# Four plain pairs instead of five in the first feed-forward block of a two-layer decoder trunk

## The reference, cut to what matters

```
def rms_norm(x, gain):
    y = xf * lax.rsqrt(jnp.mean(xf * xf, axis=-1, keepdims=True) + RMS_EPS)
    return (y * gain)
def swiglu(x, w_gate, w_up, w_down):
    return (jax.nn.silu(x @ w_gate) * (x @ w_up)) @ w_down
x = x + FFN_RESIDUAL * swiglu(rms_norm(x, g[0]), ffn_w_gate[layer, 0], ffn_w_up[layer, 0], ffn_w_down[layer, 0])
```

## Time and profile before

| | |
|---|---|
| median of 3 runs | 1962.5 us (1962.04 to 1962.67) |
| the profiled execution | 1962.62 us, span 1960.9 us |
| TensorE busy | 1949.4 us, 99% of the span |
| VectorE busy | 1396.1 us, 71% |
| ScalarE busy | 852.6 us, 43% |
| GpSimd busy | 525.8 us, 27% |
| the chain that ended last | TensorE 93%, VectorE 3% |

### The profile page before, as it was taken

The page is one execution under the profiler, slowest core; times in us unless marked ns, Lnnn a source line. Parts: engine busy times, 40 slices in busy tenths (PEclk is TensorE's granted clock), DMA queues, the critical chain, the costliest instruction groups (busy, mean ns, idle before and its releaser), DMA issues.

```text
span 1960.9 us, 28973 instructions
## 1 busy us (share of the span) xinstructions
PE 1949.4 (99%) x11722; PEld 1707.9 (87%) x11722; DVE 1396.1 (71%) x1881; ACT 852.6 (43%) x1231; POOL 525.8 (27%) x394
## 2 busy tenths in 40 slices
PE   9999999999999999999999999999999999999999
PEld 7999998877789999988999998877777888999997
DVE  8877776554578777768877786773458567877873
ACT  6443333535564333445433344442546345333431
POOL 1322222152222222223322322200015413322221
PEclk9999999999999999999999999999999999999999
DMA  6566663351336666534666653222200235666653
GB/s 214 151 167 167 173 170 98 119 172 54 101 117 168 168 174 166 161 119 134 178 172 171 177 158 113 97 91 91 76 1 1 86 108 162 175 179 165 179 143 106
DMA packets 110229, 265.92 MB, mean 136 GB/s; under 512 B 10129, under 2 KB 18577, under 8 KB 110097
## 3 DMA queue, kind: packets, MB, share of 16 engines
q1 hardware_dynamic: 90096, 225.72, 34.9%
q0 software_dynamic: 19856, 38.28, 12.4%
q10 hardware_dynamic: 144, 0.09, 0.0%
HBM read 259.32 MB, written 4.72 MB: 135 GB/s over the span
## 4 chain that ended last, share of the span: by engine, by line
PE 93%; DVE 3%; ACT 1%; issue 1%; DMA 1%; POOL 0%; SPq 0%; DVEq 0%
PE BANKS L657 12%; PE BANKS L659 12%; PE BANKS L658 12%; PE BANKS L579 10%; PE BANKS L581 10%; PE BANKS L580 10%; PE BANKS L710 6%; PE BANKS L711 6%; PE BANKS L712 6%; PE BANKS L1023 2%; PE BANKS L851 1%; PE BANKS L853 1%; PE BANKS L852 1%; PE BANKS L1000 1%; PE BANKS L814 1%
## 5 line engine op out<-in xcount | busy, mean ns | idle before, releaser
L579 PE MATMUL BANKS<-XH,HI 128*128 128x512 f32 x624 | 245.9, 394 | 3.9 <-DVE LO L1652 1.9
L657 PE MATMUL BANKS<-BF,ASH 128*128 128x256 f32 x876 | 248.0, 283 | 0.0
L658 PE MATMUL BANKS<-BFL,ASH 128*128 128x256 f32 x876 | 247.9, 283 | 0.0
L659 PE MATMUL BANKS<-BF,ASL 128*128 128x256 f32 x876 | 247.9, 283 | 0.0
L1652 DVE TENSOR_TENSOR LO<-RING,HI 128x1024 fp32r<-128x1024 f32 (+2 forms) x204 | 215.0, 1054 | 42.1 <-ACT HI L1159 40.7
L580 PE MATMUL BANKS<-XL,HI 128*128 128x512 f32 x624 | 243.2, 390 | 0.0
L581 PE MATMUL BANKS<-XH,LO 128*128 128x512 f32 x624 | 243.1, 390 | 0.0
L1172 ACT ACTIVATE TMP<-TMP 128x512 f32<-128x512 f32 x88 | 55.7, 633 | 411.8 <-DVE TMP L1681 411.8
L2251 POOL TENSOR_TENSOR TMP<-TMP,RSTD 128x512 f32<-128x512 f32 x88 | 131.4, 1493 | 365.3 <-ACT TMP L1172 365.3
L2243 POOL DMA_DIRECT2D ASR<-gu_dram x73 | 88.1, 1219 | 398.4 <-DMA ASR<-gu_dram 391.9
L710 PE MATMUL BANKS<-HH,DHI 128*128 128x512 f32 x496 | 194.0, 391 | 0.1
(11 more groups left out here) (249 smaller groups left out, 4866.4 us busy)
## 6 DMA issues: line engine op xcount, KB each, us to landing
RING<-gu_dram SPq DMA_DIRECT2D x174, 512.0 KB, 3.6
ASR<-gu_dram SPq DMA_DIRECT2D x146, 256.0 KB, 2.9
ASR<-gu_dram POOLq DMA_DIRECT2D x73, 512.0 KB, 6.8
DRAW<-down_dram SPq DMA_DIRECT2D x48, 512.0 KB, 3.7
RING<-oin_dram SPq DMA_DIRECT2D x32, 512.0 KB, 3.5
RING<-down_dram SPq DMA_DIRECT2D x32, 384.0 KB, 3.2
RING<-ein_dram SPq DMA_DIRECT2D x16, 512.0 KB, 3.5
RING<-oout_dram SPq DMA_DIRECT2D x16, 512.0 KB, 3.5
```

The source lines that it names most:

```text
L579: pe.matmul(PS[bank][:], HI[j][:, c], hi(k), start=(n == 0), stop=False)
L657: pe.matmul(out, w_hi[:, c], x_hi(k), start=(k == 0), stop=False)
L658: pe.matmul(out, w_hi[:, c], x_lo(k), start=False, stop=False)
L659: last = pe.matmul(out, w_lo[:, c], x_hi(k), start=False, stop=(k == 3))
```

## The change

`PLAIN[0]` goes from 5 to 4: pair 4 becomes a block pair, the forms, the weight sums and the first early part are wanted one pair sooner, and the early parts follow pairs 4 to 19 in place of 5 to 20. The written lists of ScalarE and VectorE for f == 0 lose one plain pair and are put into another order, near that of block 1. The lists of SyncE, GpSimd and TensorE follow from `PLAIN`.

```diff
-PLAIN = (5, 4, 3, 3)
+PLAIN = (4, 4, 3, 3)
@@ ScalarE, f == 0
                     form_split(f, 1)
                     h_high(0)
+                    split(7, whole)
                     silu(1, 1.0)
-                    split(7, whole)
                     form_inputs(f, 3)
                     form_split(f, 2)
+                    sums_split(first, 0)
+                    form_split(f, 3)
                     h_high(1)
-                    split(8, whole)
+                    split(2 * first, whole)
                     silu(2, 1.0)
-                    form_split(f, 3)
                     h_high(2)
-                    split(9, whole)
-                    sums_split(first, 0)
-                    silu(3, 1.0)
-                    split(2 * first, whole)
-                    h_high(3)
@@ VectorE, f == 0
                     split(6, whole)
-                    up(0)
                     form(f, 2)
                     form_split(f, 1)
+                    up(0)
+                    split(7, whole)
                     gate(1)
-                    split(7, whole)
-                    up(1)
                     form(f, 3)
                     form_split(f, 2)
-                    gate(2)
-                    split(8, whole)
                     form_split(f, 3)
-                    up(2)
-                    gate(3)
-                    split(9, whole)
+                    up(1)
                     sums_second(first)
                     sums_third(first)
-                    up(3)
+                    gate(2)
+                    up(2)
```

## The result

The changed kernel takes **1968.13 us** (median of 8 runs, 1967.25 to 1968.63), the kernel before beside it on the same chip 1962.62 us (median of 8 runs, 1962.04 to 1963.28). The ratio is 1.0027, 95% interval 1.0018 to 1.0036: slower by 5.5 us. The forecast was 1967.7. The profiled execution took 1968.36 us, its span is 1966.5 us; those of before took 1962.62 and 1960.9.

What follows compares the result with a forecast made beforehand. TensorE, busy in 99% of the span, was taken as the bound. The terms -0.8 + 3.75 + 0.25 + 0.85 + 1.1 = +5.15 us, on a median of 1962.5, gave 1967.7 us, range 1964.5 to 1970.3.

Steps and rivals of the forecast that it cites:

- The trade, -0.8: TensorE, pair 4 of block 0: 84 block-pair matmuls (10.07 us) replace 48 plain ones (10.88), worth -0.8 us.
- Unit 7, +3.75: Block 0: TensorE waits for VectorE's up(1) until 49.65 instead of 46.00, +3.65, plus 0.1 for a slower first matmul.
- the effect at 1.2: VectorE and GpSimd lock: taking them as independent would get form(2) below 1.2 us earlier, the first stall 1.2 smaller.
- Block start +0.25: Block 0's first block pair: TensorE waits for the up tile's split, until 55.35, +0.25 us with the slower first matmul.
- second product +0.85: Block 0's first block pair: second product waits for the first sums' split, ending at 57.65, +0.85 us.
- last product +1.1: Block 0's first block pair: last product starts at 66.05, set by gate(3) and a 7.41 us chain, +1.1 us.
- The clock as a rival, 1970.1: Clock falls to 1.2 GHz in the stall, unit 7's matmuls cost 2.4 us more: 1970.1 us; chance 0.12.
- the prediction's own last line: Wrong if unit 7 starts within 1 us of 46.0, the clock leaves full level, or loss lies behind 75 us.
- Block 1's price: Rival: block 0 only pays waits like block 1's at unit 7 and last product, 2.2 in all: 1963.9 us; chance 0.15.
- no stall: Rival: VectorE is never held up, up(1) ends at 44.4, only the trade is left: 1961.7 us; chance 0.07.
- The backlog: Rival: VectorE, some 4 us behind, makes the next block pair wait too, up to 1 us: 1968.7; chance 0.08.
- No further waits: TensorE, behind the first block pair's last product: no further waits up to 350 us; block 0 ends about 5 us later.

Runs made afterwards that it cites:

- experiment 4: The changed kernel with 14 matmuls, whose output nobody reads, put into TensorE's stall ahead of block 0's unit 7: 1968.01 us, ratio 1.0028.
- experiment 2: The kernel before with four plain pairs in block 0, its lists in their old order without pair 4's entries: 1969.62 us, ratio 1.0033.
- experiment 1: The changed kernel with VectorE's up(1) moved directly behind gate(1), ahead of form(3) and two form splits: 1969.37 us, ratio 1.0037.
- experiment 6: The changed kernel with block 0's ScalarE and VectorE lists reordered and mid sums ahead of the early split in all blocks: 1963.92 us, ratio 1.0005.
- experiment 7: As experiment 6, but mid sums ahead of the early split in blocks 0 and 1 only: 1962.62 us, ratio 0.9998.
- experiment 3: The kernel before (five plain pairs) with only VectorE's up(1) moved back, behind form(3) and form_split(2): 1964.42 us, ratio 1.0007.
- experiment 9: The kernel before with mid sums first in blocks 0 and 1, and block 1's unit 7 split ahead of h_high(1) and up(1): 1960.15 us, ratio 0.9983.
- experiment 5: The changed kernel with VectorE's mid sums ahead of the early weights' split in every block's first block pair: 1967.66 us, ratio 1.0024.

## Why the prediction was right

Term by term, by the prediction's own steps:

- **The trade, -0.8.** Not to be seen alone, but block 0's sum closes with it: -0.8, + 3.62 and the slower first matmul (0.1) for unit 7, + 1.61 for the low clock, + 0.56 for the last product (65.98 against 56.78 + 6 x 1.44 = 65.42) gives 5.09, as measured.
- **Unit 7, +3.75.** Right, step for step: `up(0)` was put at 38.75 and came at 38.68, `gate(1)` 42.5 and 42.41, `up(1)` 48.9 and 48.79, unit 7 49.65 and 49.62. It took the turns of VectorE and GpSimd to get there: the form's first row at 35.01 lasts 1.0 longer than one without them (1.48 against 0.47), where the prediction put the effect at 1.2.
- **Block start +0.25, second product +0.85, last product +1.1.** Together 2.2, measured 1.61 + 0.56 = 2.17, but by another course. The first two are not there; the low clock stands in their place and takes half of the third. That it only stands in for them is shown by experiment 4, which waits at the block's start until 55.32 (worked out: 55.35), at the second product until 57.56 (57.65) and at the last until 65.97 (66.05), and takes the same time. The three terms were never three costs: they are the distance from TensorE's own pace to `gate(3)` (58.57; 58.65 was worked out) and the 7.41 us behind it, paid in pieces.
- **The clock as a rival, 1970.1.** Its mechanism happened: the clock fell behind the stall and stayed at half for 3.4 us. The Trainium skill's page "TensorE: Matmul & The Clock Gate", section "HAM oscillation — how this bites in real kernels", warns that idle gaps of TensorE bring the low clock back; the trace agrees, by the window at 50.90. By the prediction's own last line this was a sign of being wrong, and the forecast did not have it. That the number held all the same has a reason and a piece of luck: the low clock cost 1.6 us, and 2.2 us of slack happened to lie behind it. The rival's price was wrong. I added 2.4 us to a sum that had VectorE as its bound up to the last product; anything TensorE loses ahead of that product, up to 2.2 us, is free. In experiment 2, where TensorE restarts at 56.86 with the block's 72 matmuls ahead, the low clock makes TensorE the bound again: 56.86 to 67.27 is 10.41 us for 8.64 us of matmuls, `mid_five` is done at 66.35, and 0.9 us of that run's loss is the clock's: TensorE comes to the last product that much behind its input.
- **Block 1's price and no stall** fell with the stall of 3.45 us. "No stall" needed `up(1)` 3.6 us sooner; the two idle times of VectorE (1.65 and 1.72) are the serial handovers that stood against it. Experiment 1 adds that an `up(1)` so early would have saved nothing by itself. Against block 1's price the prediction counted two forms and four splits behind the reciprocal's first `gate`; VectorE's timeline of the changed kernel has three and six there, which speaks against that rival all the more. **The backlog** fell too: behind the first block pair only the 0.33 us at the second one's early part (83.26) follow, and the kernel before has them as well.
- "No further waits" and the time of all other blocks were right to 0.4 us; that piece is block 1's unit 7, which I took for fixed at 0.71 and which isn't.

What the prediction did not ask is how much of the loss can be had back: experiments 6 and 7 show that, given four plain pairs, 4.3 to 4.6 of the 5.1 us come from the order of the lists, the `mid` sums' place among them. Nor did it ask what the old order would cost there; experiment 2 says 1.0 more in block 0, nearly all of it the low clock's 0.9.

## What to carry to other kernels

When a unit of work moves ahead on the bounding engine, walk the in-order lists of the helper engines to the *last* join that they feed, and take the stalls ahead of it as parts of one delay, not as costs to be added or removed one by one: taking the first wait away gives nothing where the next join hangs on the same list (experiment 1), and costs or gives its whole length where that list has room (experiment 3). The same holds for a slow clock behind a stall. The gain lies in idle time inside the helper's list: put an instruction whose input is ready ahead of one that waits for another engine (experiment 9, the split ahead of `up(1)`).

## What the runs showed of the hardware

- The granted clock did not fall while TensorE stood for 3.6 us but behind the restart, at 50.9 after a restart at 49.62, and was full again at 54.3. The same stall in experiment 5 (restart at 49.63) had the clock low from 50.2 to 53.6. In the longer waits of experiments 1 and 2 (4.96 and 5.19 us) it fell while TensorE still stood, at 56.5 and at 53.9, and was low from the first matmul on, whose row takes 0.58 where the same row behind a short wait takes 0.39 (experiment 6). The waits of up to 1.57 us in these runs left it full.
- With 14 matmuls of 0.23 us in the 3.6 us (experiment 4) it stayed full throughout, and the time was the same: here the low clock ran in time that TensorE would have waited. In experiment 2, where TensorE was the last to be ready, it cost 0.9 us.
- The turns of VectorE and GpSimd fall elsewhere when a wait moves. VectorE's weight sum took 1.78 at 49.73 in experiment 1, beside GpSimd's HL(1), and 0.68 at 49.39 in the changed kernel, where GpSimd begins only at 50.22: the price of an order can't be read off its instruction counts.
- Left open: what sets block 1's wait at unit 7 (0.71, 1.11, none, 1.57 with the same lists).
